# Context first, with its gathered rows in the samples' mixer; 320 dense tokens; mixer weights in a ring of four slots

## What is computed

```python
def layer(x, mod, conv_fn, C0, n0, m0, ...):
    sh1, sc1, g1, sh2, sc2, g2 = mod
    hin = rmsnorm(x) * (1 + sc1) + sh1
    mix, state = token_mixers(hin, ...)      # u, v_s, q|k, v, o, gates = hin @ w_in; conv, gMLP, two-way mLSTM; @ w_out
    x = x + g1 * mix
    hin = rmsnorm(x) * (1 + sc2) + sh2
    return x + g2 * peer(hin, ...), state

def peer(h, w_pq, sub_keys, expert_u, expert_v):
    qh = (t @ w_pq).reshape(T, 8, 2, 128)                        # 8 heads
    s_top, i_top = lax.top_k(einsum('thpd,hpkd->thpk', qh, sub_keys), 16)
    best, pos = lax.top_k(s_top[:, :, 0, :, None] + s_top[:, :, 1, None, :], 16)   # 16 of 16384 experts a head
    act = gelu(einsum('td,thkd->thk', tb, expert_u[ib]))
    return einsum('thk,thkd->td', softmax(best) * act, expert_v[ib])
```

## Time and profile before

| | |
|---|---|
| median of 3 runs | 3629.84 us (3628.98 to 3630.05) |
| span of the profiled execution | 3624.5 us |
| outside the span, against the median | 5.3 us |
| layer 1, first loop product at | 695 us |
| layer 2, from its first transpose | 1856 us |
| layer 2, first dense query | 2203 us |
| layer 2, last dense key scores end | 2300 us |
| layer 2, first one-hot group on PE | 2364 us |
| layer 2, first loop product | 2462.6 us |

### The profile page before, as it was taken

One profiled execution on the slowest core, in us unless ns is written; L12 is line 12 of the kernel. 1 busy time (PEld: TensorE's weight loads), 2 busy tenths in 40 slices (PEclk: granted clock), 3 DMA queues, 4 the chain that ended last, 5 costly groups with the idle time before them and its releaser, 6 DMA issues. The chain is left out here.

```text
span 3624.5 us, 44749 instructions
## 1 busy us (share of the span) xinstructions
PE 3549.4 (98%) x15394; PEld 2491.2 (69%) x15394; DVE 2634.7 (73%) x5798; ACT 545.8 (15%) x1123; POOL 1819.4 (50%) x1615
## 2 busy tenths in 40 slices
PE   7999999999999999999999999999999999999998
PEld 3445568777777777777765456787777777777776
DVE  4523589997888777777766355999888877777777
ACT  3212214500000000000021131171000000000001
POOL 0011007776676566666501200387667756666673
PEclk9999999999999999999999999999999999999999
DMA  9821203899999999999961003069999999999998
GB/s 396 311 75 55 105 26 103 314 416 409 418 418 419 376 418 419 419 419 419 416 224 41 30 30 119 12 232 387 414 415 419 418 405 388 419 419 419 419 419 317
DMA packets 344842, 1114.47 MB, mean 307 GB/s; under 512 B 34320, under 2 KB 81552, under 8 KB 343424
## 3 DMA queue, kind: packets, MB, share of 16 engines
q0 software_dynamic: 175104, 637.61, 43.5%
q1 hardware_dynamic: 166240, 465.71, 33.1%
q10 hardware_dynamic: 3360, 9.57, 0.7%
HBM read 1067.63 MB, written 45.07 MB: 307 GB/s over the span
## 5 line engine op out<-in xcount | busy, mean ns | idle before, releaser
L1551 PE MATMUL ps<-big,y_nat 128*128 128x336 f32 x4032 | 1180.8, 447 | 1.9 <-ACT gates_area L1669 1.9
L1551 PEld LDWEIGHTS ps<-big,y_nat 128*128 128x128 f32 x4032 | 763.5, 190 | 327.4 <-issue 2.3
L2164 POOL DMA_INDIRECT big<-in_peer_u,gates_area x512 | 665.9, 1301 | 360.4 <-DVE kn_area L1942 227.6
L1960 DVE SCALAR_TENSOR_TENSOR big<-big,kn_area 128x1024 f32<-128x1024 f32 x608 | 784.5, 1290 | 24.5 <-DMA big<-in_peer_v,gates_area 18.1
L1942 DVE CUSTOM_DVE_ANT_0 big<-big,y_nat 128x1024 f32<-128x1024 f32 x608 | 739.8, 1223 | 19.8 <-DMA big<-in_peer_u,gates_area 16.1
L2175 POOL DMA_INDIRECT big<-in_peer_v,gates_area x512 | 566.7, 1107 | 296.9 <-DVE big L1960 171.1
L1564 PEld LDWEIGHTS ps<-gates_area,y_nat 128*128 128x128 f32 x2048 | 363.9, 190 | 61.1 <-issue 61.1
L1564 PEld LDWEIGHTS ps<-gates_area,big 128*128 128x128 f32 x2048 | 363.9, 190 | 61.1 <-issue 61.1
L1564 PE MATMUL ps<-gates_area,y_nat 128*128 128x208 f32 x2048 | 381.1, 340 | 0.0
L1564 PE MATMUL ps<-gates_area,big 128*128 128x208 f32 x2048 | 381.1, 340 | 0.0
L589 PE MATMUL ps<-big 128*128 128x512 f32 x640 | 282.1, 596 | 0.0
(11 more groups left out here) (307 smaller groups left out, 3530.6 us busy)
## 6 DMA issues: line engine op xcount, KB each, us to landing
y_nat<-in_peer_ut SPq DMA_DIRECT2D x256, 512.0 KB, 6.6
y_nat<-in_peer_v SPq DMA_DIRECT2D x128, 512.0 KB
big<-in_peer_v SPq DMA_DIRECT2D x128, 512.0 KB
big<-in_w_mod SPq DMA_DIRECT2D x24, 2048.0 KB, 14.6
expert_gates<-big SPq DMA_DIRECT2D x10, 3584.0 KB, 13.2
gates_area<-expert_gates SPq DMA_DIRECT2D x32, 560.0 KB
big<-expert_gates SPq DMA_DIRECT2D x32, 560.0 KB
big<-in_w_in SPq DMA_DIRECT2D x8, 2048.0 KB, 15.4
```

Source lines behind the costliest of these rows:

```text
L1551: last = pe.matmul(ps[:, 6 + par, 0:NX], u_s[par][:, k, :], h_t[:, k, X0:ND], start=(k == 0), stop=(k == KD - 1))
L1960: dve.scalar_tensor_tensor(out=acc, in0=v_ring[:, k % VSLOTS, :], scalar=wact[:, k:k + 1], in1=acc, op0=ALU.mult, op1=ALU.add).then_inc(s_ ...
L2164: pool.indirect_dma_start(out=u_ring[k % USLOTS], out_offset=None, in_=io["peer_u"][:, :], in_offset=bass.IndirectOffsetOnAxis(ap=rows_at( ...
```

## The change

1. **Order.** The context goes alone first: its norm, gates, q/k (L837 in the new file, 128 columns), v, v_s, u, o, mLSTM, output (L942), second norm, queries (L966), key scores (L980) and choice of experts (DVE and POOL, one tile). Four of the samples' q/k blocks (`qk_s`, L899) lie between its steps on PE. Then the samples' mixer follows with 512 tokens.
2. **Gathered rows in the mixer.** 70 of a layer's gathered operations (QE) are done by DVE at named points of the samples' mixer (`early(label)`, table `EARLY`, one row for each layer), with their indirect DMAs on POOL and the activation of each dot on ACT. A ring has four places there (SHALLOW) and eight in the loop (DEEP). The loop starts with the context's rows; only tile 3 is chosen in the loop, from step 2.
3. **320 dense tokens.** X0 = 64 tokens of tile 0 are gathered, in two parts; 20 units, so 640 gathered operations a layer, 570 of them in the loop. A step on PE is 8 of 128x320, 2 of 128x512 and 8 of 128x192. There are 40 one-hot groups in place of 42, and eight gate blocks in place of six.
4. **Queries.** Dense queries as before; tile 3's alone are left behind them (L1215, 128 columns).
5. **Weights.** SBUF is one `arena`. The mixer's weights and the queries' go through four slots of 1 MB in the order of the list ORDER; w_in and w_out are loaded twice in a layer, wq three times. The modulation weights have four pieces of their own. The samples' x is stored to DRAM between the layers and loaded again by tile for the output additions.

The core of the diff:

```diff
-XB, XA = 32, 16
-X0 = XB + XA
+XB = 64
+X0 = XB
 NX = ND - X0
-PARTS, SHARES = P // XB, P // XA
+PARTS = P // XB
 MOVED = 2 * P - X0
-USLOTS, VSLOTS = 8, 8
 OCT = 8
-BLOCKS = 6
+BLOCKS = 8
...
-FIRST_AT, NEXT_AT = 0, 24
...
+OPS = 2 * UNITS * TOPK
+NEXT_AT = 2
...
+SHALLOW, DEEP = 4, 8
+
+LABELS = ("ranked", "j4", "j5", "j6", "j7", "p0", "p1", "p2", "p3", "g0", "g1", "g2", "g3", "c0", "c1", "c2", "m0", "m1", "m2", "m3")
+EARLY = [dict(zip(LABELS, counts)) for counts in (
+    (0, 0, 0, 0, 0, 8, 14, 20, 26, 31, 36, 41, 46, 50, 54, 58, 61, 64, 67, 70),
+    (10, 12, 14, 16, 18, 21, 24, 27, 30, 34, 38, 42, 46, 50, 54, 58, 61, 64, 67, 70))]
...
-    begun = HIDDEN + BY_STEP * max(0, min(j, STEADY) - 1)
-    steps = range(STEADY, N_KEYS - 1)
     load = lambda s: 2 if s - NEXT_AT in HEAVY else 5
-    return begun + (2 * UNITS * TOPK - HIDDEN - BY_STEP * (STEADY - 1)) * sum(load(s) for s in steps if s < j) // sum(load(s) for s in steps)
...
+    steps = range(N_KEYS - 1)
+    return QE + (OPS - QE) * sum(load(s) for s in steps if s < j) // sum(load(s) for s in steps)
...
+            ORDER = [("mod", p) for p in range(4 if first else 0)]
+            ORDER += [("qk_c", m) for m in range(4)] + [("proj_c", i) for i in range(8)] + [("qk_s", 0)]
+            ORDER += [("out_c", i) for i in range(4)] + [("qk_s", 1)] + [("q_c", m) for m in range(8)]
+            ORDER += [("proj_s", 0), ("proj_s", 1), ("qk_s", 2), ("qk_s", 3)] + [("proj_s", i) for i in range(2, 8)]
+            ORDER += [("out_s", i) for i in range(4)] + [("q_s", m) for m in range(8)] + [("q_l", m) for m in range(8)]
...
+                    def early(label):
+
+                        for q in range(done[0], EARLY[l][label]):
+                            gathered(q)
+                        done[0] = EARLY[l][label]
...
+                    gmlp_mean(v16, sq16, ms2, s_sv)
+                    early("g0")
+                    gmlp_norm(v16, ms2, rs2, ST * HEADS, s_sa, sa("gmlp_root"), s_sv)
+                    early("g1")
+                    early("g2")
+                    early("g3")
+                    dve.wait_ge(s_pe, 3 * ST)
+                    for h in range(HEADS):
+                        dve.wait_ge(s_kt, ST + h + 1)
+                        yv = ua[:, :, h * DH:(h + 1) * DH]
```

More of the change, by code:

```diff
@@ L98, in gathered_op, with place_of, landed, last_in @@
     return "add", p - 1, (r - 1) // 2
-VA = DH + 1
+DOTS_EARLY = sum(gathered_op(q)[0] == "dot" for q in range(QE))
+ADDS_EARLY = QE - DOTS_EARLY
+def place_of(n, done):
+    shallow = done + SHALLOW
+    while n >= shallow + DEEP - SHALLOW:
+        n -= DEEP
+    return n % SHALLOW if n < shallow else SHALLOW + n - shallow
+U_PLACE = [place_of(n, DOTS_EARLY) for n in range(UNITS * TOPK)]
+V_PLACE = [place_of(n, ADDS_EARLY) for n in range(UNITS * TOPK)]
+def landed(place, l, n):
+    return 16 * (l * place.count(place[n]) + place[:n + 1].count(place[n]))
+def last_in(place, n):
+    before = [m for m in range(n) if place[m] == place[n]]
+    return before[-1] if before else None
 class Lane:
@@ new lines, in mod_columns, with mods @@
+                    def mod_columns(j):
+                        pe.wait_ge(s_mrow, 1 + 4 * (j + 1))
+                        pe.wait_ge(s_const, 9)
+                        for n in range(2):
+                            last = pe.transpose(ps[:, MOD_BANKS[j], NQ + n * P:NQ + (n + 1) * P], mrow[:, j % 2, n * P:(n + 1) * P], ident[:, :])
+                        last.then_inc(s_mcol, 1)
+                    def mods(products, columns=None):
+                        if first and columns is not None:
+                            mod_columns(columns)
+                        if first and products is not None:
+                            mod_products(products)
@@ new lines, in _ @@
+                    if first:
+                        mod_products(0)
+                        mod_columns(0)
+                        mod_products(1)
+                        mod_columns(1)
+                        pe.wait_ge(s_xn, 1)
+                    for k in range(KD):
+                        last = pe.transpose(bank(4 + k // 4, k % 4 * P, (k % 4 + 1) * P), row_c[:, k * P:(k + 1) * P], ident[:, :])
+                        if k % 4 == 3:
+                            last.then_inc(s_cp, 1)
@@ new lines, in _, with mixed_c @@
+                    qk_s(0)
+                    def mixed_c(part, src):
+                        pe.wait_ge(*((s_cv, cv("gmlp_done")) if part == 0 else (s_cv, cv("mixed"))))
+                        if part == 1:
+                            pe.wait_ge(s_ca, ca("mixed_t", 1))
+                        for h in range(HEADS):
+                            last = pe.transpose(bank(3, h * P, (h + 1) * P), src[:, h * P:(h + 1) * P], ident[:, :])
+                        last.then_inc(s_cp, 1)
+                    pe.wait_ge(s_ht, KD)
@@ new lines, in out @@
+                    def out(t, half):
+                        n = 2 * t + half
+                        if n == 0:
+                            pe.wait_ge(s_pe, 4 * ST)
+                        if n >= 2:
+                            pe.wait_ge(s_t5, n - 1)
+                        pe.wait_ge(s_ye, 2 * t + 2)
+                        for kh in range(2):
+                            w = weights("out_s", 2 * half + kh)
+                            for k in range(4):
+                                last = pe.matmul(bank(half), yT[t % 2][:, 4 * kh + k, :], w[:, k, :], start=(kh == 0 and k == 0), stop=(kh == 1 and k == 3))
+                        last.then_inc(s_o5, 1)
```

3014 lines of the change are left out of this document (1687 added, 1327 removed).

## The result

The changed kernel takes 3879.04 us (3869.43 to 3888.18), 1.0688 times the kernel before (interval 1.0674 to 1.0701): slower by 250 us, where +30 was forecast in a range that ended at +85. Its profiled execution has a span of 3875.5 us.

The account below looks back on a forecast made before the run. PE columns bound the loop, with DMA at its limit too; the mixer had free DMA and DVE. Layers of +16 and +18 us on 3624.5 gave 3658.5, with 5.3 around it 3664, less 4 for overlap 3660; range 3576 to 3715.

Parts of the forecast that it names:

- The loop: Expert loop: steps fall from 9.05 to 8.61 us, DVE and DMA (417 GB/s) both fit, 55 us gained a layer.
- Rival B: Loop keeps its pace because DMA is at its limit: step 8.8 instead of 8.61, loops lose 48 us, 3708; chance 0.08.
- The sum: Whole kernel: layer 2 +16 and layer 1 +18 us, 34 on the profiled execution's 3624.5.
- The choice of experts: Before the one-hot groups: PE idle about 25 us waiting for DVE's 59 us chain; stretch only 3 us shorter.
- The slow start behind that idle time: One-hot groups: a cold start of PE's clock after 25 us of idle time, not carried in the sum.
- One-hot groups: Two fewer groups save 4 us a layer, and less gate storing behind the last group saves 2.
- The samples' mixer: Layer 2, up to the first dense query: +75 us, of it 34 moved, 3 splitting, 38 new waits.
- The convolutions: Samples' mixer, layer 2: intra-chunk scores need the last convolution, so PE waits some 13 us for DVE.
- 38 + 7: Layer 2's mixer: 38 us of PE waits beyond those of before, which were about 7.
- its +2: Layer 1's mixer against layer 2's: DVE late by about 16 and 19 us instead of 0 and 11; together +2.
- Rival A: Mixer waits are absorbed by DVE's 158 us of free time: faster, 3586 to 3606 us; chance 0.30.
- Rival C: Weight ring starves PE: 24 context pieces 1 us late each, 24 us a layer, 3708; chance 0.15 with D.

Follow-up runs that it names:

- u_whole: Changed kernel with the even steps' u block loaded, from step 4 on, to 1024 contiguous words a partition, not eight pieces of h_t: 3735.09 us, 1.0295.
- before_cut: Kernel before, with the even steps' u block loaded in two halves of 256 KB in 512-byte pieces: 3767.75 us, 1.0384.
- its control: Kernel before, with the even steps' u block loaded in the same two halves of 256 KB, but in contiguous 2 KB pieces: 3629.99 us, 1.0001.
- tile3_alone: Kernel before, with the context's queries and key scores left out behind the dense ones and tile 3's scores used for both: 3621.02 us, 0.998.
- none_early: u_whole with none of the 70 early operations in the samples' mixer, all 640 gathered operations of a layer in the loop: 3839.86 us, 1.0583.
- spread: u_whole with all 70 early operations moved to other places in the samples' mixer: 3703.55 us, 1.0216.
- moved_early: u_whole with 51 early operations for 70, at places where DVE is idle: 3716.93 us, 1.0245.

## Why the prediction was wrong

**The loop: the step that failed.** "Both fit, the DMA with nothing to spare. I take 55." The PE part was exact (8.62 us, 4.30 + 1.72 + 2.60). The DMA part divided bytes by the rate of before, as if a byte had one price. That rate was measured with whole blocks; every second u block came in packets of 512 bytes. Shown by u_whole and, in the other kernel, by before_cut with its control. Rival B named the right resource ("it takes only a few per cent more bytes or worse interleaving to lose some") but with a chance of 0.08 and a price of 48 us; the pieces were not in it, and they cost 141 us in the two loops (the table's after against u_whole). Without the pieces u_whole still misses the 55 by 11 us a layer: "both fit" was wrong there too, by little. The sum asked for 417 GB/s against the 419 of before, and this kernel's loop moved 410. (Two terms of the 3.59 MB were off and cancel: the gates are 560 KB in four steps, 0.14 MB a step and not 0.2, and outside the four light steps, which have two fifths of the rows of a full one, the code asks for 570/(123 + 4 x 0.4) = 4.58 rows, not 4.45.) Why this kernel moves 410 where the one before moves 419 stays open.

**The choice of experts: right.** Forecast 25 us of idle PE, 3 us gained; measured 23.5, and 5 to 6 gained. tile3_alone shows the mechanism by itself. The slow start behind that idle time, which the prediction named and left out, is there: the first 96 records took 14.09 us, 147 ns each for the 119 of the earlier trace rows, at a granted clock of 0.69 (2595 to 2605).

**One-hot groups: right.** 6 us a layer forecast; measured 100.0 to 93.3 and 98.1 to 93.7.

**The samples' mixer: most places right, sizes low.** The first dense query of layer 2 came at 2438.8 - 1987.15 = +451.7 from the first transpose, forecast +421. PE's waits in it:

```profile
2056.86 7.03 PE L899 MATMUL ps<-arena 128*128 128x512 f32 x16
...
2086.88 9.96 PE L899 MATMUL ps<-arena 128*128 128x512 f32 x16 [6.40 <-DMA arena<-in_w_in]
...
2201.19 9.11 PE L899 MATMUL ps<-arena 128*128 128x512 f32 x16 [15.22 <-DVEq L1962]
...
2227.98 2.04 PE L1043 MATMUL ps<-arena 128*128 128x128 f32 x8 [7.74 <-DVEq L1962]
...
2299.13 3.78 PE L1071 MATMUL ps<-arena,mixw 128*128 128x512 f32 x4 [12.00 <-DVE arena L2283]
...
2342.16 1.20 PE L1103 MATMUL ps<-arena 128*128 128x258 f32 x2 [5.80 <-DVEq L2311]
...
2359.90 1.12 PE L1123 MATMUL ps<-ident,arena 128*128 128x128 f32 x4 [8.43 <-DVEq L2391]
```

At the gMLP products it is 12.0 (forecast 11), at the states 5.8 (6), at the tail 8.4 (12). The convolutions took 15.2 + 7.7 = 22.9, forecast 13, because DVE's choice for the context ended later and the first rows landed later:

```profile
2167.41 0.29 DVE L2101 TENSOR_SCALAR arena<-arena,exp_base 128x128 uint32<-128x128 f32 x1
2175.41 1.23 DVE L2152 CUSTOM_DVE_ANT_0 arena<-arena 128x1024 f32<-128x1024 f32 x1 [7.71 <-DMA arena<-in_peer_u,arena]
...
2194.39 0.75 DVE L1947 TENSOR_SCALAR arena<-ps,convw 128x512 f32<-128x512 f32 x1
```

The choice ended at +180.5, not +170, ten dots took until +207, not +189. A weights wait of 6.4 us (q/k block 2, the ring) was put at 2. And behind two of these waits matmuls are longer, 9.96 and 9.11 for 7.03; the clock granted between 2137 and 2438 was 0.91 and 0.90 on average, between the two levels of 1.2 and 2.4 GHz (the windows, columns as above):

```profile
2137.00:2285.00 148.00, 123.68 (x340) 58.90 (x339) 110.86 (x212) 24.53 (x38) 74.38 (x61) 0.91 0.62 213
2285.00:2438.00 153.00, 121.10 (x388) 67.39 (x386) 104.22 (x231) 33.56 (x79) 58.52 (x45) 0.90 0.57 197
```

Five us a layer were taken for that and for late rows. The waits shown in this stretch, 6.4 + 15.2 + 7.7 + 12.0 + 5.8 + 8.4, are 55.5 us, where the sum had 38 + 7; the other 14 of layer 2's 24 us of miss are longer matmuls and small waits, which no run separates. none_early divides the miss another way. The sum had 24 us of waits at the early operations' places in layer 2 (13 and 11) and, by its +2, 26 in layer 1; the run shows 46 and 43. Without them the sum leaves 56 us for the context's path in each layer; the run shows 58 and 72. So in layer 2 it is the early operations that were priced too low, and in layer 1 both. In layer 1 PE waits 17.5 us at the gMLP products (19 forecast) and 19.1 for ACT's copies of the projections (L1472), which stand behind ACT's own waits for POOL's part of the score weighting; what makes the context's path 16 us longer there stays open.

Rival A (absorbed) fell: none_early shows that the early operations cost 43 to 46 us a layer and spread that other places save 10 and 20. Rival C (the ring) is there with one wait of 6.4 us in each layer, at the samples' q/k block 2.

**The sum.** +34 forecast; 83.2 and 79.4 more in the loops and 30.2 and 24.3 more ahead of them make 251, the difference of the spans.

No version beat the kernel before. The best of this form, spread, is at 1.0216; it has gained its 44 us a layer in the loop and pays 90 and 72 ahead of it.

## What to carry over

When a buffer moves, look at the shape of its new place as well as at its size: a transfer of the same bytes into eight pieces a partition can cost a DMA-bound loop more than the work that the change took away. Price a saturated DMA by packets and bytes, look at whether the consumers of its rows wait even while PE is full, and where a sum says "fits with nothing to spare", give the rival its real weight. And before work is moved out from beside another engine's chain, read which of the two ends last: 28 us of matmuls a layer were worth 4.

## What was not expected of the hardware

- A 512 KB block in pieces of 512 bytes cost 0.92 to 1.16 us more than in pieces of 4 KB, beside gathered traffic at 370 to 388 GB/s in all; in pieces of 1 KB at least 0.15, in pieces of 2 KB nothing that could be measured.
- The share of the DMA engines does not show it: 1.01 at 385 GB/s with small pieces, 1.03 at 410 and 419 without. A full share at a lower rate is the sign.
- Waits of 2.8 to 3.3 us in the full loop were followed by sixteen matmuls of 4.57, 6.26 and 7.36 us for 4.47: nearly the same idle time costs nothing more, or almost as much again.
- With only large packets in the streams, u_whole, moved_early and none_early move 409 to 410 GB/s at a share of 1.03 and wait for rows, though they ask for different amounts, while the kernel before moves 419. Why their rows can't come faster stays open.
